# High and low parts of a weight unit side by side: a weight read at a stride of 8 bytes

## The chip, the cores and the metric

The kernel runs on one NeuronCore of a Trainium2 chip. The metric is the device time of one execution in microseconds. TensorE does the matmuls, VectorE, ScalarE and GpSimd prepare their operands and take over their results, and SyncE starts the DMAs.

## The reference

A two-layer encoder trunk works on two sequences of 256 tokens with 1024 features, 512 tokens in all, which share the weights. In fp32, each layer computes

```
h = x + 1/2 * SwiGLU(RMSNorm(x))            # feed-forward, 1024 -> 2816 -> 1024
u = RMSNorm(h); p = u @ w_in                # 28 tiles of 128 columns
A = retention(4 heads), B = differential attention(4 heads)
h = h + concat(A, B) @ w_out
h = h + 1/2 * SwiGLU(RMSNorm(h))            # second feed-forward
x = RMSNorm(h)
```

with `SwiGLU(x) = (silu(x @ wg) * (x @ wu)) @ wd`. Everything is fp32, and the result is compared as such. Nearly all the work is the products with weights.

## The kernel before

Activations lie transposed in SBUF: 128 features on the partitions, tokens along the row. A weight *unit* is 128 output columns times up to 8 tiles of 128 input rows, that is 128 partitions x 1024 words, 512 KB. Units stream in by DMA from SyncE's queue, in a written order, into four raw buffers (`raw`, and `raw_x` in the feed-forwards).

TensorE multiplies in the fast form fp32r, which rounds its operands. So each operand is split into a high part (the rounded value) and a low part (the rest), and each weight tile takes three matmuls, in `three` (L785 to L790): high weight times high moving tile (L788), high weight times low moving tile (L789), low weight times high moving tile (L790). Each of them loads its 128 x 128 weight tile anew, during the matmul before it. ScalarE writes the high part with a Copy from fp32 to fp32r; GpSimd or VectorE subtracts it from the raw value and writes the low part.

There are two kinds of units. *Plain* units are used in the first four products of each feed-forward, in its last down projection, in the 28 projections and in `w_out`. ScalarE splits one in L1276 and GpSimd in L679, in two halves. Most of their matmuls have 512 moving columns; the last products of the kernel are done for 256 tokens at a time, with 256 columns. *Fast blocks* make up the rest of the feed-forwards: 28 in each of four. A block takes two units (two gate/up units or two down units) as a 2 x 2 block matrix and computes it with seven half-size products instead of eight, p1 to p7, each of 4 tiles x 3 matmuls of 256 columns: 84 matmuls. For this the engines form sums and differences of weight quarters: per block, GpSimd runs L688 (low part of the first unit), L698 and L700 (differences of quarters, in place), L713 (low part of one quarter) and L706 (low part of two differences). ScalarE writes high parts in L1293, L1301, L1307, L1323 and L1330; VectorE writes two low parts in L1881. In some blocks GpSimd also runs L720, which concerns no weight.

Each engine's order is written out by hand, with semaphores between them. In GpSimd's order for block b come L713 and L706 of block b + 1 and then L688, L698 and L700 of block b + 2. L706 waits for L1301, which waits for L700 of its block. ScalarE's copies wait until TensorE has finished with the slot that they overwrite.

Split weights lie in slots. Slots 0 to 3 are in `w`, slots 4 and 5 in `w_x`; a fast block uses slots 0, 1, 2 or 3, 4, 5, alternately. `w_tiles` gives the high and low part of a slot: today two dense areas, the low part `W_PART` or `X_PART` words behind the high one, with the fourth slot 64 words further on (`SPACER`). Plain units begin 8 words (`PLAIN_AT`) later than the units of fast blocks (`block_tiles`). Moving operands are dense, with 256 or 512 words read in a row.

Of the kernel before, what the change touches and what calls it, by code (L numbers as in the profile page):

```python
# [30 lines left out]
F32R = mybir.dt.float32r  # L31
# [4 lines left out]
P = 128  # L36
# [18 lines left out]
UT = 8  # L55
SLOTS = 4
# [5 lines left out]
KH = KD // 2  # L62
PLAIN_AT = 8
SPACER = 64
W_AT = (0, UT * P, 2 * UT * P, 3 * UT * P + SPACER)
W_PART = SLOTS * UT * P + SPACER
X_PART = 2 * UT * P
GAP = 56


# [135 lines left out]
def build(nc, x, w_gu, w_dn, w_p, w_o, par, lam_vec, table, one_hot, cossin, rel, ident_in, centre_in, y):  # L206
    with ExitStack() as ctx:
        def sb(name, shape, dt=F32):
            return ctx.enter_context(nc.sbuf_tensor(name, shape, dt))
# [12 lines left out]
        a_lo = sb("a_lo", [P, UT, T], F32R)  # L222
        raw = sb("raw", [P, RAW * UT * P])
        pr = sb("pr", [P, N_PAR])
        w = sb("w", [P, 2 * W_PART + PLAIN_AT], F32R)
        acc = sb("acc", [P, T])
        rms = sb("rms", [P, T])
        cs = sb("cs", [P, 2, T])
# [21 lines left out]
        with ExitStack() as ffn_only:  # L250
            def sb_ffn(name, shape, dt=F32):
                return ffn_only.enter_context(nc.sbuf_tensor(name, shape, dt))

            raw_x = sb_ffn("raw_x", [P, RAW * UT * P])
            w_x = sb_ffn("w_x", [P, 2 * X_PART + PLAIN_AT], F32R)
            mix_hi = sb_ffn("mix_hi", [P, 3, KH, SEQ], F32R)
            mix_lo = sb_ffn("mix_lo", [P, 3, KH, SEQ], F32R)
            up = sb_ffn("up", [P, T])
            p1_copy = sb_ffn("p1_copy", [P, SEQ])
            u2 = sb_ffn("u2", [P, SEQ])  # L260
            u43 = sb_ffn("u43", [P, 2, SEQ])
            s14_h = sb_ffn("s14_h", [P, JS, T], F32R)
            s14_l = sb_ffn("s14_l", [P, JS, T], F32R)
            s2_h = sb_ffn("s2_h", [P, JS, SEQ], F32R)
            s2_l = sb_ffn("s2_l", [P, JS, SEQ], F32R)
# [225 lines left out]

        def w_tiles(s, n=UT, at_=0, shift=PLAIN_AT):

            buffer, part, first = (w, W_PART, W_AT[s]) if s < SLOTS else (w_x, X_PART, (s - SLOTS) * UT * P)
            first += shift + at_ * P
            hi, lo = buffer[:, first:first + n * P], buffer[:, part + first:part + first + n * P]
            return hi.rearrange("p (a b) -> p a b", b=P), lo.rearrange("p (a b) -> p a b", b=P)

        def block_tiles(s, n=UT, at_=0):

            return w_tiles(s, n, at_, 0)

        def w_tile(s, k):
            return w_tiles(s, 1, k)[0][:, 0, :]

        def w_low_tile(s, k):
            return w_tiles(s, 1, k)[1][:, 0, :]
# [1972 lines left out]
```

## Time and profile before

| | |
|---|---|
| median of 3 runs | 1840.61 us (1840.57 to 1845.08) |
| profiled execution | 1838.56 us, of which the span is 1836.8 us |
| TensorE busy | 99% of the span, 12744 matmuls |
| weight loads | 92% |
| VectorE, GpSimd, ScalarE busy | 75%, 73%, 55% |
| granted TensorE clock | 0.999 |
| DMA | 186.73 MB, 102 GB/s on average |

Busy times are unions of records. Records of matmuls overlap, since a matmul's record reaches to the end of its passage through the array; so the rate of TensorE is read from the distance between the starts of two matmuls, not from the mean duration of one.

### The profile page before, as it was taken

The numbers are of one execution on the slowest core, as the hardware profiler recorded it, in microseconds if no ns is written. First come the engines' busy times: TensorE is split into PE (matmuls) and PEld (weight loads), VectorE is DVE, ScalarE is ACT, GpSimd is POOL, SyncE is SP. The second block draws the span as 40 slices with busy tenths as digits, with TensorE's granted clock in tenths as the row PEclk, the third lists the DMA queues.
The fourth block names the chain that finished last, engine by engine and source line by source line (L and its number), as shares of the span: only waits on it lengthen the run. The fifth ranks groups of instructions, "written<-read, shape, count | busy, mean of one in ns | idle before, by whom it ended". The sixth has DMA issues, their size and how long they took to land. (4 is left out here: it accounts for less than half of the span.)

```text
span 1836.8 us, 33605 instructions
## 1 busy us (share of the span) xinstructions
PE 1822.8 (99%) x12744; PEld 1691.9 (92%) x12744; DVE 1375.7 (75%) x2409; ACT 1017.8 (55%) x1770; POOL 1348.4 (73%) x880
## 2 busy tenths in 40 slices
PE   9999999999999999999999999999999999999998
PEld 8999999887888999999889999998778889999997
DVE  7888886656755887887688888767477468888874
ACT  7656555456435665655575465555564266555553
POOL 6999897455445898988479998955544368999883
PEclk9999999999999999999999999999999999999999
DMA  4433333222223233323234233323222133333332
GB/s 153 151 110 122 115 118 107 85 99 69 69 69 114 72 114 115 108 101 110 80 110 139 96 112 116 100 86 115 80 69 70 58 115 98 110 116 106 102 113 72
DMA packets 56461, 186.73 MB, mean 102 GB/s; under 512 B 6600, under 2 KB 10440, under 8 KB 56300
## 3 DMA queue, kind: packets, MB, share of 16 engines
q1 hardware_dynamic: 54000, 181.09, 29.5%
q10 hardware_dynamic: 2300, 3.48, 0.5%
q8 instruction: 102, 1.67, 0.4%
q14 instruction: 59, 0.48, 0.1%
HBM read 182.44 MB, written 3.15 MB: 101 GB/s over the span
## 5 line engine op out<-in xcount | busy, mean ns | idle before, releaser
L788 PE MATMUL bank<-hg_hi,w 128*128 128x256 f32 (+1 forms) x1396 | 441.8, 317 | 0.1
L789 PE MATMUL bank<-hg_lo,w 128*128 128x256 f32 (+1 forms) x1396 | 438.3, 314 | 0.0
L790 PE MATMUL bank<-hg_hi,w 128*128 128x256 f32 (+1 forms) x1396 | 438.0, 314 | 0.0
L679 POOL TENSOR_TENSOR w<-raw,w 128x512 fp32r<-128x512 f32 (+1 forms) x194 | 259.1, 1358 | 217.7 <-ACT w L1276 217.6
L788 PEld LDWEIGHTS bank<-hg_hi,w 128*128 128x128 f32 x1396 | 262.2, 188 | 19.8 <-issue 2.7
L790 PEld LDWEIGHTS bank<-hg_hi,w 128*128 128x128 f32 x1396 | 262.3, 188 | 17.6
L789 PEld LDWEIGHTS bank<-hg_lo,w 128*128 128x128 f32 x1396 | 262.3, 188 | 16.9
L1356 ACT ACTIVATE bank<-bank 128x512 f32<-128x512 f32 x88 | 51.1, 581 | 237.5 <-DVE bank L1938 237.5
L1276 ACT ACTIVATE w<-raw 128x1024 fp32r<-128x1024 f32 (+1 forms) x97 | 98.8, 1023 | 120.6 <-PE bank L790 95.6
L706 POOL TENSOR_TENSOR w<-raw_x,w 128x1024 fp32r<-128x1024 f32 x56 | 135.0, 2411 | 26.2 <-ACT w L1301 26.2
L688 POOL TENSOR_TENSOR w<-raw_x,w 128x1024 fp32r<-128x1024 f32 x56 | 136.1, 2430 | 15.9 <-ACT w L1293 15.4
L706 POOL TENSOR_TENSOR w_x<-raw,w_x 128x1024 fp32r<-128x1024 f32 x56 | 135.2, 2414 | 14.0 <-ACT w_x L1301 14.0
L788 PE MATMUL bank<-a_hi,w 128*128 128x256 f32 (+1 forms) x472 | 139.7, 296 | 0.2 <-DVE a_lo L1865 0.2
L789 PE MATMUL bank<-a_lo,w 128*128 128x256 f32 (+1 forms) x472 | 139.0, 295 | 0.0
L790 PE MATMUL bank<-a_hi,w 128*128 128x256 f32 (+1 forms) x472 | 139.0, 294 | 0.0
L688 POOL TENSOR_TENSOR w<-raw,w 128x1024 fp32r<-128x1024 f32 x56 | 136.6, 2439 | 0.0
L788 PE MATMUL bank<-mix_hi,w_x 128*128 128x256 f32 x480 | 134.2, 280 | 2.1 <-DVE u L1907 2.1
L788 PE MATMUL bank<-mix_hi,w 128*128 128x256 f32 x480 | 134.1, 279 | 1.0 <-DVE w L1881 0.5
L789 PE MATMUL bank<-mix_lo,w 128*128 128x256 f32 x480 | 134.2, 279 | 0.0
L789 PE MATMUL bank<-mix_lo,w_x 128*128 128x256 f32 x480 | 134.2, 279 | 0.0
L790 PE MATMUL bank<-mix_hi,w 128*128 128x256 f32 x480 | 134.1, 279 | 0.0
L790 PE MATMUL bank<-mix_hi,w_x 128*128 128x256 f32 x480 | 134.0, 279 | 0.0
(345 smaller groups left out, 5824.2 us busy)
## 6 DMA issues: line engine op xcount, KB each, us to landing
raw<-in_w_gu SPq DMA_DIRECT2D x96, 512.0 KB, 4.0
raw_x<-in_w_gu SPq DMA_DIRECT2D x80, 512.0 KB, 4.3
raw<-in_w_p SPq DMA_DIRECT2D x56, 512.0 KB, 3.3
raw_x<-in_w_dn SPq DMA_DIRECT2D x32, 512.0 KB, 4.1
raw<-in_w_dn SPq DMA_DIRECT2D x32, 512.0 KB, 4.2
raw<-in_w_o SPq DMA_DIRECT2D x16, 512.0 KB, 3.3
raw_x<-in_w_dn SPq DMA_DIRECT2D x16, 384.0 KB, 3.9
raw<-in_w_dn SPq DMA_DIRECT2D x16, 384.0 KB, 3.5
```

What stands on the lines that cost most here:

```text
L679: ins = pool.tensor_tensor(columns(lo_[:, part, :]), source[:, part.start * P:part.stop * P], columns(hi[:, part, :]).bitcast(F32), ALU.su ...
L688: pool.tensor_tensor(columns(lo_), raw_tiles(RAW_AT["t", m, 0], UT), columns(hi).bitcast(F32), ALU.subtract).then_inc(g_lo, 1)
L706: pool.tensor_tensor(columns(lo_).rearrange("p (a b) -> p a b", a=2), both, columns(hi).rearrange("p (a b) -> p a b", a=2).bitcast(F32), A ...
L788: pe.matmul(out, hi[:, 0, :], m_hi, start=first, stop=False)
L789: pe.matmul(out, hi[:, 0, :], m_lo, start=False, stop=False)
L790: return pe.matmul(out, lo_[:, 0, :], m_hi, start=False, stop=last)
L1276: act.activation(columns(hi), raw_tiles(RAW_AT["e", e], TILES_OF[e]), ACT.Copy).then_inc(hi_done, 1)
L1356: act.activation(gated, gated, ACT.Silu).then_inc(silu_done, 1)
```

## The change

The two areas are replaced by one per slot, of 2048 words. Word 0 is the first high word, word 1 the first low word, word 2 the second high word, and so on. High and low parts become views with a step of two words. So a weight load of 128 columns reads 128 words spread over 1024 bytes, where it read 512 bytes in a row; and the Copies and subtractions that write or read these parts do it at a step of two words too. No instruction, wait or DMA is added or removed. `w` becomes 64 words shorter, so that the tensors allocated after it lie 256 bytes lower; `w_x` keeps its size, and the start of each kind of unit within 256 bytes is kept.

```diff
-W_AT = (0, UT * P, 2 * UT * P, 3 * UT * P + SPACER)
-W_PART = SLOTS * UT * P + SPACER
-X_PART = 2 * UT * P
+UNIT = 2 * UT * P
+W_AT = (0, UNIT, 2 * UNIT, 3 * UNIT + SPACER)
@@
-        w = sb("w", [P, 2 * W_PART + PLAIN_AT], F32R)
+        w = sb("w", [P, SLOTS * UNIT + SPACER + PLAIN_AT], F32R)
@@
-            w_x = sb_ffn("w_x", [P, 2 * X_PART + PLAIN_AT], F32R)
+            w_x = sb_ffn("w_x", [P, 2 * UNIT + PLAIN_AT], F32R)
@@
         def w_tiles(s, n=UT, at_=0, shift=PLAIN_AT):
-            buffer, part, first = (w, W_PART, W_AT[s]) if s < SLOTS else (w_x, X_PART, (s - SLOTS) * UT * P)
-            first += shift + at_ * P
-            hi, lo = buffer[:, first:first + n * P], buffer[:, part + first:part + first + n * P]
-            return hi.rearrange("p (a b) -> p a b", b=P), lo.rearrange("p (a b) -> p a b", b=P)
+            buffer, first = (w, W_AT[s]) if s < SLOTS else (w_x, (s - SLOTS) * UNIT)
+            first += shift + 2 * at_ * P
+            both = buffer[:, first:first + 2 * n * P].rearrange("p (a b two) -> p a b two", b=P, two=2)
+            return both[:, :, :, 0], both[:, :, :, 1]
```

## Rows read from the trace of the kernel before

**Rows 1.** The page, parts 1 and 4: engines, and the chain that ended last.
```profile
PE 1822.8 (99%) x12744; PEld 1691.9 (92%) x12744; DVE 1375.7 (75%) x2409; ACT 1017.8 (55%) x1770; POOL 1348.4 (73%) x880
...
PE 44%; DVE 0%; ACT 0%; POOL 0%; issue 0%; DVEq 0%; ACTq 0%
```

**Rows 2.** Groups by shape, TensorE: count, busy us and mean ns, idle before.
```profile
L788 PE MATMUL bank<-hg_hi,w 128*128 128x256 f32 x960 | 267.8, 279 | 0.1
L788 PE MATMUL bank<-hg_hi,w 128*128 128x512 f32 x436 | 174.0, 399 | 0.0
...
L1207 PE MATMUL bank<-s,v 128*128 128x256 f32 x64 | 15.1, 379 | 0.0
...
L788 PE MATMUL pair<-hg_hi,w_x 128*128 128x512 f32 x32 | 12.6, 393 | 0.0
...
L788 PE MATMUL pair<-hg_hi,w 128*128 128x512 f32 x32 | 12.5, 389 | 0.0
```

**Rows 3.** Windows: length; busy us (instructions) of PE, PEld, DVE, ACT, POOL; clock; DMA.
```profile
700.00:800.00 100.00, 99.98 (x857) 99.81 (x856) 81.85 (x156) 57.81 (x100) 89.91 (x55) 1.00 0.32 108
```

**Rows 4.** Timeline of TensorE in a fast block: start, duration; nine matmuls.
```profile
302.11 0.28 PE L788 MATMUL bank<-hg_hi,w 128*128 128x256 f32 x1
...
303.04 0.28 PE L790 MATMUL bank<-hg_hi,w 128*128 128x256 f32 x1
```

**Rows 5.** Timeline of TensorE in a projection; seven matmuls.
```profile
368.30 0.39 PE L788 MATMUL bank<-hg_hi,w 128*128 128x512 f32 x1
...
369.66 0.39 PE L788 MATMUL bank<-hg_hi,w 128*128 128x512 f32 x1
```

**Rows 6.** Timeline of TensorE in the last products; eleven matmuls.
```profile
1824.24 0.28 PE L788 MATMUL bank<-a_hi,w 128*128 128x256 f32 x1
...
1825.44 0.28 PE L789 MATMUL bank<-a_lo,w 128*128 128x256 f32 x1
```

**Rows 7.** Source view of L800, its load of 4 columns: min/median/max ns.
```profile
L800 PEld LDWEIGHTS bank<-a_t,o_r x2: 77/78/80, 26.7 to 26.7; 32*4 32x4 f32 x2
```

**Rows 8.** The page, part 5: weight loads of L788.
```profile
L788 PEld LDWEIGHTS bank<-hg_hi,w 128*128 128x128 f32 x1396 | 262.2, 188 | 19.8 <-issue 2.7
```

**Rows 9.** Timeline of TensorE, fp32 matmuls of the retention part, merged.
```profile
488.98 1.89 PE L1207 MATMUL bank<-s,v 128*128 128x256 f32 x8
```

**Rows 10.** The page, part 5: GpSimd's L688 and L706.
```profile
L706 POOL TENSOR_TENSOR w<-raw_x,w 128x1024 fp32r<-128x1024 f32 x56 | 135.0, 2411 | 26.2 <-ACT w L1301 26.2
L688 POOL TENSOR_TENSOR w<-raw_x,w 128x1024 fp32r<-128x1024 f32 x56 | 136.1, 2430 | 15.9 <-ACT w L1293 15.4
...
L688 POOL TENSOR_TENSOR w<-raw,w 128x1024 fp32r<-128x1024 f32 x56 | 136.6, 2439 | 0.0
```

**Rows 11.** Timeline of GpSimd over two rounds.
```profile
631.52 2.39 POOL L688 TENSOR_TENSOR w<-raw,w 128x1024 fp32r<-128x1024 f32 x1
...
636.93 0.74 POOL L720 TENSOR_TENSOR s_l<-a_t,s_h 128x256 fp32r<-128x256 f32 x1 [0.20 <-ACT s_h L1352]
...
641.26 2.41 POOL L688 TENSOR_TENSOR w<-raw_x,w 128x1024 fp32r<-128x1024 f32 x1
...
646.45 1.29 POOL L713 TENSOR_TENSOR w<-raw_x,w 128x512 fp32r<-128x512 f32 x1
648.19 2.41 POOL L706 TENSOR_TENSOR w<-raw_x,w 128x1024 fp32r<-128x1024 f32 x1 [0.44 <-ACT w L1301]
650.55 2.41 POOL L688 TENSOR_TENSOR w<-raw,w 128x1024 fp32r<-128x1024 f32 x1
```

**Rows 12.** Timeline of ScalarE in a fast block.
```profile
652.40 0.60 ACT L1330 ACTIVATE w<-bank 128x512 fp32r<-128x512 f32 x1
...
656.35 1.04 ACT L1301 ACTIVATE w_x<-raw 128x1024 fp32r<-128x1024 f32 x1
```

**Rows 13.** Groups of VectorE: L1881.
```profile
L1881 DVE TENSOR_TENSOR w_x<-bank,w_x 128x512 fp32r<-128x512 f32 x112 | 76.6, 684 | 11.9 <-ACT w_x L1323 6.1 <-ACT w_x L1330 4.4
```

## The prediction

> **What bounds the kernel now.** I read the page first: TensorE is busy for 99% of the span, and every entry of the chain that ended last is a TensorE line; no other engine has a per cent of it [rows 1]. So only two things can move the time: the distance between two matmuls, or a producer that stops keeping up. Next I read the groups by shape: almost all the work is three matmuls per weight tile at L788 to L790, in a 256-column and a 512-column form [rows 2]. Busy time says little here, since the records overlap; the distance between starts is what counts.
>
> In the timeline that distance is as regular as a clock. In the fast blocks (256 columns) eight steps take 0.93 us, and over 100 us 857 matmuls start: 116.7 ns each [rows 3, 4]. In a projection (512 columns) six steps take 1.36 us: 226.7 ns [rows 5]. In the closing products (256 columns) ten steps take 1.20 us: 120.0 ns [rows 6]. The last two use the same kind of weight unit ("plain", eight words further on), so they give the rate of the moving stream: 226.7 - 120.0 = 106.7 ns for 256 more columns, one column per cycle at the 2.4 GHz level, which is granted throughout [rows 3]. What is left is a fixed part of 13.3 ns per plain matmul, and 116.7 - 106.7 = 10.0 ns in the fast blocks. It is worth a lot: 112 fast blocks (56 + 56 calls of L688) [rows 10] x 84 matmuls = 9,408, times 10.0 ns = 94 us; about 2,700 matmuls of 512 columns (12,744 less 9,552 of 256 columns and nearly 500 others) times 13.3 ns = 36 us; and 144 at the end.
>
> **Where the fixed part comes from.** Three readings. First, fast and closing matmuls have the same number of columns and differ in where the weights start; the fixed part is 10.0 against 13.3 ns. It depends on addresses, so it is not plain issue cost. Second, a weight load of 4 columns takes 78 ns and one of 128 takes 188 [rows 7, 8]: 110 ns for 124 columns, 0.89 ns each, about two cycles. So dense weights are read at some 4.5 to 4.8 bytes per ns, while the moving operand of the fp32r form is read at 4 bytes per 0.417 ns, 9.6 bytes per ns. The moving read overtakes the weight read's address pattern again and again during each load. Third, in the fp32 matmuls of the retention part, eight records of 256 columns take 1.89 us, the last of them 0.38: 1.51 / 7 = 216 ns [rows 2, 9]. There each column takes two cycles (213.3 ns for 256), both reads advance at one speed, and the fixed part is only 2.6 ns. That the two reads of TensorE disturb each other when their addresses advance at different speeds is my reading of these three; the trace has no row for an fp32r matmul with a strided weight.
>
> **The change part by part.** *Weight reads.* Nothing is added to or removed from any queue: the same matmuls, loads, waits and DMAs in the same order. A weight read now steps 8 bytes per column, 9.0 to 9.6 bytes per ns: the speed of the moving read. If the reading above holds, a load that collides once is pushed out of step and stays clear. Best end: the fixed part falls to the 2.6 ns of the fp32 row, that is to 109.3 ns in the fast blocks and 215.9 at 512 columns: 9,408 x 7.4 ns = 70 us, 2,700 x 10.7 ns = 29 us, 144 x 10.7 ns = 1.5 us; together 100 us on TensorE alone. Worst end: a load touches twice as many bytes' worth of memory, and the fixed part doubles: 9,408 x 10.0 + 2,844 x 13.3 ns = 94 + 38 = +132 us (+163 us if the fast blocks pay 13.3 ns too). No row decides between them; the fp32 row is the nearest in kind, so I take the gain, with doubt, as the chances show.
>
> *What then comes late.* GpSimd. Where it waits only for its hand-over from ScalarE, its round of five subtractions takes 9.29 us (from the L688 at 641.26 to the next at 650.55) [rows 11], against 84 x 116.7 ns = 9.80 us of TensorE. With TensorE at 84 x 109.3 ns = 9.18 us, GpSimd's round is the longer one. Rounds that also hold the low part of a sum (8 of 28 in each feed-forward) cost about 0.5 us more: 9.74 us, from 631.52 to 641.26, with L720 inside [rows 11]. So the fast blocks of one feed-forward can't go below 28 x 9.29 + 8 x 0.45 = 263.7 us, from 28 x 9.80 = 274.4: 10.7 us, four times 43 us, instead of 70. I take 40 for these, and of the 29 us at 512 columns two thirds, 19, since the attention stages also hold waits on VectorE and ScalarE that don't shrink. With 1 us at the end: 60 us.
>
> *GpSimd's own work.* L688, L706 and L713 now read the high part and write the low part at a stride of 8 bytes; 2.43 + 2.41 + 1.29 = 6.13 us of each block [rows 10, 11]. No row here has a strided GpSimd operand. Lower end 0 (nothing that would make it cheaper: the elements are the same, about 2.35 ns each). Upper end: two of the three streams cost double, 5/3 of 6.13, +4.1 us per block; less the cover of 9.80 - 9.29 = 0.51 us, 112 x 3.6 = +400 us. I take 0, as the cost per element of these lines is already several times that of one step of ScalarE, which moves 1,024 elements in 1.04 us [rows 12], so that the address step is not what limits it. The point from which it decides: 0.51 us is 8% of 6.13; beyond that each further per cent is 0.061 x 112 = 7 us.
> The Trainium skill has a rule on this ("GPSIMD Engine Reference", section 7, Performance pitfalls for Q7 kernels): reads get half as dear again once the step exceeds 8 bytes. A step of 8 is just inside, so by that rule the cost is 0; it says nothing of writes, and no row here shows either.
>
> *ScalarE and VectorE.* L1293 and L1301 (1,024 elements, 1.04 us) and L1307, L1323 and L1330 (512, 0.60 us) write strided: 3.9 us of a block in which ScalarE is busy 58% [rows 3, 12]. L1881 reads and writes strided, 2 x 0.68 us, VectorE busy 82% [rows 3, 13]. On ScalarE 512 more elements cost 0.44 us, 0.86 ns each. I take 0; the upper end, twice the time, would put 1.04 us more of L1301 straight before L706, whose wait of 0.44 us for it is already there [rows 11]: GpSimd's round 10.33 us, less the 9.80 of TensorE, 0.53 x 112 = +59 us. The DMAs are unchanged, at a share of 0.32 [rows 3]. The weight tensor shrinks by 64 words, so all buffers behind it move by 256 bytes; units at both parities of 256 bytes exist today (w_x against w), with means of 393 and 389 ns [rows 2]; the 4 ns are the wait of a first tile, so I take 0, and as the upper end those 4 ns on all 512-column matmuls, 11 us.
>
> **Sum.** 1838.6 us (the profiled execution, 1836.8 of span) - 60 = 1778.6; the median of the runs shown is 2.0 us above the profiled one. I say 1779.
>
> **The rivals.** *A, the weight reads get dearer (slower).* The disturbance goes by the memory a load touches, not by relative speed. For it: the fixed part of plain units is 13.3 ns, 32 cycles, at 256 and at 512 columns alike, as a toll per load would be; the fp32 row can be explained by slack in its slower moving stream instead. Against it: the 10.0 ns for units only 32 bytes away. Price, as above: 1839 + 132 = 1971, up to 2002. It decides as soon as the mean distance in the fast blocks passes 116.7 ns, because TensorE has no idle time there; each further ns is 9.4 us.
> *B, nothing happens on TensorE.* The fixed part has to do with the load's start address and the switch of weights, and a step of 8 bytes is no burden. For it: the starts stay where they were, modulo 256 bytes. Against it: 116.7 and 120.0 ns for equal columns, and the 2.6 ns of fp32 [rows 4, 6, 9]. 1836 to 1841.
> The Trainium skill ("TensorE: Matmul & The Clock Gate", section Step-by-step: what each phase is for) speaks for B: TensorE has two independent read ports, one for each operand. By that there would be nothing to win or lose, 1839; the 116.7 against 120.0 ns for equal columns already speaks against full independence. "SBUF — State Buffer", section Specifications (TRN2), gives lines of 16 bytes and full rate from two hits per line; a step of 8 bytes has just two, so that rule sees no loss either, and A would contradict it.
> *C, strided producers (slower).* As bounded above; with GpSimd 20% dearer, (0.20 x 6.13 - 0.51) x 112 = +80, 1919; if TensorE wins at the same time, the same round still decides.
>
> **How the numbers follow.** Forecast 0.43, A 0.29, B 0.14, C 0.14. The forecast's own range is 1745 (GpSimd's round shortens a little as well, all of the 29 us come) to 1815 (half of the gain). Measurements of this kernel tell 0.3%, 5.5 us, from no change. Faster is the forecast, 0.43; same is B, 0.14; slower is A and C, 0.43. The range must reach into A and C: 1748 to 1975 leaves out the dearer half of A, some dear cases of C and a little below, not quite 2 in 10.
>
> **What would show it.** Distances in the fast blocks: 109 to 112 ns where GpSimd doesn't hold them up (A: 127 or more; B: 116.7). In a projection: 216 to 220 ns (A: 240; B: 226.7). Weight loads of 188 ns staying within 5. GpSimd's L706 at 2.41, L688 at 2.40 us (C: from 2.6 up), and new idle time of TensorE ended by POOL L706 or L713, with GpSimd above 95% in the fast blocks. I am wrong if TensorE's distances don't fall, or if a producer's mean rises by over 8%.

## The result, and the profile after

The changed kernel takes 1884.46 us (median of 3 runs, 1883.66 to 1884.89) against 1840.61 before: ratio 1.0239 [1.0224, 1.0253], 44 us slower. The forecast was 1779 us. The sign was wrong. The time lies inside the range of 1748 to 1975 only because that range was drawn to reach into the rivals; it is on the side of rival A, but far below A's 1971. Ratios, here and below, leave out executions that took over 1.5% more than the fastest of their kernel, which matters in E7 alone.

First the page of the changed kernel, its parts 1 and 4; the lines of the three matmuls are one earlier than before (L787 to L789).

```profile
PE 1867.8 (99%) x12744; PEld 1739.3 (92%) x12744; DVE 1380.6 (73%) x2409; ACT 1059.2 (56%) x1770; POOL 1370.6 (73%) x880
...
PE 43%; DVE 0%; ACT 0%; POOL 0%; issue 0%; DVEq 0%; ACTq 0%
```

TensorE still fills the span, so nothing has turned into a wait: the waits of TensorE that the changed kernel's trace lists are as small as before, and the two longest are these (line waited for: us in total, times, longest).

```profile
PE bank L787 <- DVE u L1906: 2.6, 3, 1.2
PE bank L851 <- ACT hg_hi L1738: 1.6, 1, 1.6
```

What grew is the distance between matmuls, from the start of one to the start of the next. The same 100 us as in [rows 3] (length; busy us and instructions of PE, PEld, DVE, ACT, POOL; clock; DMA), and the timeline of TensorE in a fast block (nine matmuls from the first row to the second), in a projection (seven) and in the last products (eleven):

```profile
700.00:800.00 100.00, 100.00 (x836) 100.00 (x835) 80.96 (x155) 57.74 (x93) 90.34 (x55) 1.00 0.32 107
```
```profile
311.33 0.28 PE L787 MATMUL bank<-mix_hi,w_x 128*128 128x256 f32 x1
...
312.29 0.29 PE L789 MATMUL bank<-mix_hi,w_x 128*128 128x256 f32 x1
...
376.17 0.40 PE L787 MATMUL bank<-hg_hi,w 128*128 128x512 f32 x1
...
377.57 0.39 PE L787 MATMUL bank<-hg_hi,w 128*128 128x512 f32 x1
...
1859.85 0.28 PE L787 MATMUL bank<-a_hi,w 128*128 128x256 f32 x1
...
1861.05 0.28 PE L788 MATMUL bank<-a_lo,w 128*128 128x256 f32 x1
```

In the fast block eight steps take 0.96 us, 120.0 ns each (before 116.7, [rows 4]); in 100 us 836 matmuls start where 857 did. In the projection six steps take 1.40 us, 233.3 ns (before 226.7, [rows 5]). In the last products ten steps take 1.20 us, 120.0 ns, just as before [rows 6]: a first hint that a stride alone is no toll on every load. Averaged over all neighbouring starts of the two traces, the distances (those under 160 and 300 ns) go from 116.9 to 120.4 ns at 256 columns and from 227.4 to 233.1 at 512: 9,408 x 3.5 + 2,700 x 5.7 ns = 33 + 15 = 48 us, against the 45 us by which the span grew (1836.8 to 1881.9). The other 3 us are the breaks in the 256-column stream: what its distances above 160 ns hold beyond the regular pace falls from 10.0 to 6.7 us, since a slower TensorE waits less. The granted clock is 0.999 before and after, so cycles and not the clock explain it.

The other rows that answer to those of before: the weight load, GpSimd's two large subtractions, ScalarE's L1301 (now L1300) and VectorE's L1881 (now L1880).

```profile
L787 PEld LDWEIGHTS bank<-hg_hi,w 128*128 128x128 f32 x1396 | 273.4, 196 | 19.5 <-issue 2.6
L705 POOL TENSOR_TENSOR w<-raw_x,w 128x1024 fp32r<-128x1024 f32 x56 | 138.2, 2467 | 30.6 <-ACT w L1300 30.6
L687 POOL TENSOR_TENSOR w<-raw_x,w 128x1024 fp32r<-128x1024 f32 x56 | 138.8, 2479 | 17.9 <-ACT w L1292 17.9
...
L1300 ACT ACTIVATE w_x<-raw 128x1024 fp32r<-128x1024 f32 x56 | 64.6, 1153 | 0.0
...
L1880 DVE TENSOR_TENSOR w_x<-bank,w_x 128x512 fp32r<-128x512 f32 x112 | 76.7, 685 | 18.6 <-ACT w_x L1329 11.5 <-ACT w_x L1322 7.2
```

A weight load takes 196 ns instead of 188 [rows 8]. GpSimd's rows grow by 2%, from 2430 and 2411 [rows 10] to 2479 and 2467; ScalarE's by 10%, from 1050 ns on average (L1301 into `w_x`) to 1153; VectorE's not at all (684 to 685, [rows 13]).

### The profile page after: what moved, and what is told of

Same layout as the page of the kernel before. It is cut to its first block and busy times, and to the rows that moved or that the text cites. A ratio compares the mean times of both kernels' runs of the same rounds, so it can differ in the third digit from the quotient of the medians.

```text
span 1881.9 us, 33605 instructions
## 1 busy us (share of the span) xinstructions
PE 1867.8 (99%) x12744; PEld 1739.3 (92%) x12744; DVE 1380.6 (73%) x2409; ACT 1059.2 (56%) x1770; POOL 1370.6 (73%) x880
## 5 line engine op out<-in xcount | busy, mean ns | idle before, releaser
L787 PE MATMUL bank<-hg_hi,w 128*128 128x256 f32 (+1 forms) x1396 | 449.1, 322 | 0.0
L788 PE MATMUL bank<-hg_lo,w 128*128 128x256 f32 (+1 forms) x1396 | 445.2, 319 | 0.0
L789 PE MATMUL bank<-hg_hi,w 128*128 128x256 f32 (+1 forms) x1396 | 445.0, 319 | 0.0
L678 POOL TENSOR_TENSOR w<-raw,w 128x512 fp32r<-128x512 f32 (+1 forms) x194 | 266.4, 1398 | 223.4 <-ACT w L1275 223.2
L787 PEld LDWEIGHTS bank<-hg_hi,w 128*128 128x128 f32 x1396 | 273.4, 196 | 19.5 <-issue 2.6
L789 PEld LDWEIGHTS bank<-hg_hi,w 128*128 128x128 f32 x1396 | 273.2, 196 | 17.2
L788 PEld LDWEIGHTS bank<-hg_lo,w 128*128 128x128 f32 x1396 | 273.4, 196 | 16.6
L1275 ACT ACTIVATE w<-raw 128x1024 fp32r<-128x1024 f32 (+1 forms) x97 | 107.1, 1109 | 125.8 <-PE bank L789 98.6
L705 POOL TENSOR_TENSOR w<-raw_x,w 128x1024 fp32r<-128x1024 f32 x56 | 138.2, 2467 | 30.6 <-ACT w L1300 30.6
L687 POOL TENSOR_TENSOR w<-raw_x,w 128x1024 fp32r<-128x1024 f32 x56 | 138.8, 2479 | 17.9 <-ACT w L1292 17.9
L705 POOL TENSOR_TENSOR w_x<-raw,w_x 128x1024 fp32r<-128x1024 f32 x56 | 138.0, 2465 | 18.0 <-ACT w_x L1300 16.4
L787 PE MATMUL bank<-a_hi,w 128*128 128x256 f32 (+1 forms) x472 | 142.2, 301 | 0.0
L788 PE MATMUL bank<-a_lo,w 128*128 128x256 f32 (+1 forms) x472 | 141.4, 299 | 0.0
L789 PE MATMUL bank<-a_hi,w 128*128 128x256 f32 (+1 forms) x472 | 141.3, 299 | 0.0
L787 PE MATMUL bank<-mix_hi,w_x 128*128 128x256 f32 x480 | 136.8, 285 | 1.7 <-DVE u L1906 1.7
L787 PE MATMUL bank<-mix_hi,w 128*128 128x256 f32 x480 | 136.9, 285 | 0.9 <-POOL w L705 0.6
L789 PE MATMUL bank<-mix_hi,w 128*128 128x256 f32 x480 | 136.7, 285 | 0.0
L788 PE MATMUL bank<-mix_lo,w 128*128 128x256 f32 x480 | 136.6, 285 | 0.0
L789 PE MATMUL bank<-mix_hi,w_x 128*128 128x256 f32 x480 | 136.6, 285 | 0.0
L788 PE MATMUL bank<-mix_lo,w_x 128*128 128x256 f32 x480 | 136.6, 285 | 0.0
```

What stands on the lines that cost most here:

```text
L678: ins = pool.tensor_tensor(columns(lo_[:, part, :]), source[:, part.start * P:part.stop * P], columns(hi[:, part, :]).bitcast(F32), ALU.su ...
L687: pool.tensor_tensor(columns(lo_), raw_tiles(RAW_AT["t", m, 0], UT), columns(hi).bitcast(F32), ALU.subtract).then_inc(g_lo, 1)
L705: pool.tensor_tensor(columns(lo_).rearrange("p (a b) -> p a b", a=2), both, columns(hi).rearrange("p (a b) -> p a b", a=2).bitcast(F32), A ...
L787: pe.matmul(out, hi[:, 0, :], m_hi, start=first, stop=False)
L788: pe.matmul(out, hi[:, 0, :], m_lo, start=False, stop=False)
L789: return pe.matmul(out, lo_[:, 0, :], m_hi, start=False, stop=last)
```

## The experiments

All starts are those of the weights, in words modulo 64 (256 bytes), counted from where the moving operands start. Before the change the plain units start at 0 and the fast blocks' at 56; the change keeps both. Except in the two kernels of measurements, an edit is shown against the kernel before (E4 to E8) or against the changed one (E1 to E3, E9); times are medians, beside 1839.6 to 1841.5 us for the kernel before on the same chips.

### The reads measured by themselves (M1)

One line per case, 32 matmuls each, with the number of columns, the weights' start and step and the moving operand's step as its only variables; then Copies and subtractions alone. It ran once, with a granted clock of 1.00 over the first 440 us of its span, where all cases of TensorE used here lie.

```diff
+for i in range(REP): pe.matmul(acc[:, 0:256], wts(64, 1, 1), mv[:, 0:256], start=True, stop=True)
+for i in range(REP): pe.matmul(acc[:, 0:256], wts(120, 1, 1), mv[:, 0:256], start=True, stop=True)
+for i in range(REP): pe.matmul(acc[:, 0:256], wts(64, 2, 1), mv[:, 0:256], start=True, stop=True)
+for i in range(REP): pe.matmul(acc[:, 0:256], wts(64, 1, 1), mvs(256, 2), start=True, stop=True)
```

> This kernel computes nothing of the reference; it measures the disputed cost by itself. TensorE runs 70 settings of 32 equal fp32r matmuls each, 256 or 512 moving columns, with the weight read at a step of 1, 2, 3, 4 or 8 words and its start moved by 0 to 56 words against the moving operand, in some settings the moving operand at a step of 2 words; nothing else runs. Then ScalarE, GpSimd and VectorE copy or subtract 1024 elements at steps of 1 and 2 words, alone, and ScalarE once more beside TensorE. Theory 'toll' (a load that walks over more memory holds the moving read up longer, wherever it starts): at step 2 all eight starts give about 233 ns at 512 columns and 120 ns at 256, at step 4 and 8 clearly more (over 245 and 130), dense 226.7 and 116 to 120. Rival 'phase' (the fixed part goes by the distance of the two addresses): at step 2 the starts differ among themselves by more than 5 ns and at least one is at or below the best dense one (226.7 and 116.7). Rival 'relative speed', the one of the prediction: the smallest distance at every moving step comes where the weight step is twice the moving one's speed in words, so moving step 2 with weight step 4 is faster than with 1 or 2. ScalarE at a write step of 2: 1.15 us against 1.04 alone as well, if the stride costs; 1.04 if it was only the company of the other engines. GpSimd 2.47 against 2.41 with either the read or the write strided.

Its timeline of TensorE gives one row per case (start, time of all 32, line). 256 columns with dense weights at start 0 and 56; weights at step 2, start 0 and 56; step 3; step 4; then the moving operand at step 2 with weights at step 1, 2 and 4:

```profile
28.46 4.07 PE L74 MATMUL acc<-mv,wt 128*128 128x256 f32 x32
...
58.14 3.98 PE L88 MATMUL acc<-mv,wt 128*128 128x256 f32 x32
...
62.31 4.09 PE L90 MATMUL acc<-mv,wt 128*128 128x256 f32 x32
...
92.41 4.09 PE L104 MATMUL acc<-mv,wt 128*128 128x256 f32 x32
...
126.72 5.80 PE L120 MATMUL acc<-mv,wt 128*128 128x256 f32 x32
...
138.72 7.72 PE L124 MATMUL acc<-mv,wt 128*128 128x256 f32 x32
...
170.92 7.50 PE L132 MATMUL acc<-mv,wt 128*128 128x256 f32 x32
...
178.62 7.60 PE L134 MATMUL acc<-mv,wt 128*128 128x256 f32 x32
...
186.43 7.89 PE L136 MATMUL acc<-mv,wt 128*128 128x256 f32 x32
```

A row holds 31 distances and the last matmul's own passage, so 0.10 us between two rows is 3.2 ns per matmul; the distances below are those of the last 16 matmuls of a row. Dense, 256 columns: 120.0 at start 0, 116.7 at 56. Step 2: 120.0 at both. So the isolated read shows what the kernel showed, without any producer. The low parts of the changed kernel start one word after the high ones; M1 has that start as well (65), and it takes 120.0 ns too. The forecast's theory falls on the last three rows: with the moving operand at step 2, weights at step 4 are the slowest (236.5 ns), and weights at the same step 2 (230.0) are slower than dense ones (226.7). The expectation had put the match at step 4, for a moving read of one column per cycle. It takes two (226.7 ns for 256 columns), so the equal speed is at step 2; neither helps. Rival A's doubled toll falls too: at 256 columns step 2 adds 0 to 3.3 ns and not 10. At 512 columns it adds 6.6 ns at start 0 (226.7 to 233.3), nothing at 56 (233.4 both) and takes 3.3 off at 16 (233.3 to 230.0). The cost does come, but only past step 2: 173.4 ns at step 3, 233.4 at step 4.

The groups of weight loads in the same run, for step 1 (L88), 2 (L90), 3 (L120) and 4 (L124), and the subtractions of GpSimd: dense, one operand read at step 2, result written at step 2, both, read at step 3; last the Copies of ScalarE: 1,024 elements dense, written at step 2, and 512 elements dense, written at step 3 and 4.

```profile
L88 PEld LDWEIGHTS acc<-mv,wt 128*128 128x128 f32 x32 | 3.8, 188 | 0.0
...
L90 PEld LDWEIGHTS acc<-mv,wt 128*128 128x128 f32 x32 | 3.9, 196 | 0.0
...
L120 PEld LDWEIGHTS acc<-mv,wt 128*128 128x128 f32 x32 | 5.6, 261 | 0.0
...
L124 PEld LDWEIGHTS acc<-mv,wt 128*128 128x128 f32 x32 | 7.6, 330 | 0.0
```
```profile
L61 POOL TENSOR_TENSOR sc<-src,sc 128x1024 fp32r<-128x1024 f32 x4 | 9.3, 2337 | 564.2 <-ACT sc L234 564.0
L62 POOL TENSOR_TENSOR sc<-src,sc 128x1024 fp32r<-128x1024 f32 x4 | 9.5, 2369 | 0.3
L63 POOL TENSOR_TENSOR sc<-src,sc 128x1024 fp32r<-128x1024 f32 x4 | 9.4, 2342 | 0.3
L64 POOL TENSOR_TENSOR sc<-src,sc 128x1024 fp32r<-128x1024 f32 x4 | 9.6, 2388 | 0.3
L65 POOL TENSOR_TENSOR sc<-src,sc 128x1024 fp32r<-128x1024 f32 x4 | 10.3, 2573 | 0.3
```
```profile
L224 ACT ACTIVATE sc<-src 128x1024 fp32r<-128x1024 f32 x4 | 4.2, 1056 | 526.6 <-PE acc L214 526.5
L225 ACT ACTIVATE sc<-src 128x1024 fp32r<-128x1024 f32 x4 | 4.5, 1116 | 0.1
L231 ACT ACTIVATE sc<-src 128x512 fp32r<-128x512 f32 x4 | 2.5, 629 | 0.1
L226 ACT ACTIVATE sc<-src 128x512 fp32r<-128x512 f32 x4 | 3.5, 877 | 0.1
L227 ACT ACTIVATE sc<-src 128x512 fp32r<-128x512 f32 x4 | 4.4, 1100 | 0.1
```

The producers' stride costs GpSimd 2% (2337 to 2388) and ScalarE 6% (1056 to 1116); VectorE's four cases take 1225 to 1226 ns all. Beside a busy TensorE the Copy pays the same 6% (1059 to 1126 ns). A cost of 2% on GpSimd is below the 8% from which rival C decides.

### The layout without the stride (E1), and the stride in one kind of unit (E2, E3)

E1 keeps the change's one area per slot but puts high and low part densely behind each other in it. E2 does so where `shift == 0`, the fast blocks, so that only plain units are interleaved; E3 does it where `shift != 0`.

```diff
 buffer, first = (w, W_AT[s]) if s < SLOTS else (w_x, (s - SLOTS) * UNIT)
+if True:                      # E2: shift == 0, E3: shift != 0
+    first += shift + at_ * P
+    hi, lo = buffer[:, first:first + n * P], buffer[:, UT * P + first:UT * P + first + n * P]
+    return hi.rearrange("p (a b) -> p a b", b=P), lo.rearrange("p (a b) -> p a b", b=P)
```

> The changed layout with one thing undone: each slot still has one area of 2048 words and every buffer lies where the change put it, but within the slot the high part is 1024 dense words and the low part the 1024 behind them. If the stride costs (toll, phase): back to the kernel before, 1841 us within 5, distances 116.7, 226.7 and 120.0 ns, ScalarE's L1301 at 1.05 us. If the move of the later buffers by 256 bytes costs: it stays near 1884 us.

> Only the plain units are interleaved, fast blocks are dense within their slots. Toll: 512-column matmuls at 233.3 ns, +5.8 ns on 2,700, +16 us and some more at their breaks: 1857 us. If the sum of this and the next run falls short of the change's 44 us, the layouts of the two kinds interact. Phase says the same here.

> Only the units of the fast blocks are interleaved. 9,408 matmuls at about 120 to 121 ns instead of 116.9, +28 to +34 us: 1870 us. If ScalarE's or GpSimd's dearer strided work were the cause and not TensorE's reads, TensorE would show idle time ended by L1301's or L706's line, and the 512-column stages of the run before would be free.

| | time, us | ratio | distance at 512, 256 columns, ns |
|---|---|---|---|
| E1 | 1839.82 | 1.0005 [0.9996, 1.0015] | 227.4, 117.1 |
| E2 | 1856.00 | 1.0088 [1.0073, 1.0103] | 233.1, 117.1 |
| E3 | 1869.68 | 1.0163 [1.0148, 1.0178] | 227.4, 120.5 |

(Distances are means over neighbouring starts of each trace.) Moving the buffers costs nothing. At the starts that the kernel uses, the stride costs 16 us in the plain units and 30 us in the fast blocks, together 46 against the 44 of both at once, and each kind of unit changes its own distance only. E3's row for the window of [rows 3]:

```profile
700.00:800.00 100.00, 100.00 (x829) 100.00 (x828) 79.76 (x152) 58.78 (x94) 89.70 (x54) 1.00 0.31 106
```

### Every start (M2)

M1 left a doubt: the dense distances themselves moved with the start, from 116.7 to 120.0 and from 226.7 to 234.3 ns. So a second kernel, which like M1 computes nothing of the reference, goes through all 64 dense starts and the even starts at step 2, 30 matmuls each, in the kernel's order of three.

```diff
+for i in range(10): [pe.matmul(acc[:, 0:256], a, m, start=True, stop=True)
+    for a, m in ((wts(80, 1), mv[:, 0:256]), (wts(80, 1), mv[:, 512:768]), (wts(1104, 1), mv[:, 0:256]))]
```

> Computes nothing of the reference. TensorE runs 192 settings of 30 fp32r matmuls in the kernel's own order (high weight x high, high weight x low, low weight x high), dense weights at each start from 0 to 63 words modulo 64 and step-2 weights (high and low interleaved) at each even start, for 256 and 512 moving columns. If the distance goes by the start (phase): dense at 512 columns has its minimum of 226.7 ns near start 0 and lies at 231 to 234 elsewhere, dense at 256 its minimum near 56; step 2 lies between 230 and 234, and between 118 and 122, with no start as good as the best dense one. If instead every setting of one step is alike within 1 ns, the start doesn't matter and the toll is the stride's own.

It ran once too, with a granted clock of 1.00. Timeline of TensorE, 30 matmuls a row: 256 columns dense at start 0, 16 and 56; step 2 at start 20. Then 512 columns: dense at 0, 39 and 56; step 2 at 0 and 26.

```profile
27.64 3.84 PE L66 MATMUL acc<-mv,wt 128*128 128x256 f32 x30
...
91.50 3.67 PE L98 MATMUL acc<-mv,wt 128*128 128x256 f32 x30
...
251.13 3.74 PE L178 MATMUL acc<-mv,wt 128*128 128x256 f32 x30
...
323.85 3.81 PE L214 MATMUL acc<-mv,wt 128*128 128x256 f32 x30
```
```profile
413.06 7.08 PE L258 MATMUL acc<-mv,wt 128*128 128x512 f32 x30
...
702.17 7.55 PE L336 MATMUL acc<-mv,wt 128*128 128x512 f32 x30
...
828.95 7.24 PE L370 MATMUL acc<-mv,wt 128*128 128x512 f32 x30
888.25 7.24 PE L386 MATMUL acc<-mv,wt 128*128 128x512 f32 x30
...
984.68 7.15 PE L412 MATMUL acc<-mv,wt 128*128 128x512 f32 x30
```

| distance, ns | best | mean of the starts | worst | at the start that the kernel uses |
|---|---|---|---|---|
| 256, dense | 113.3 (13, 16, 19, 22, 42) | 118.3 | 121.1 (6) | 116.9 (56) |
| 256, step 2 | 118.3 (60) | 120.1 | 123.3 | 120 (56) |
| 512, dense | 226.7 (0, 30, 33) | 232.6 | 243.3 (39) | 226.7 (0) |
| 512, step 2 | 229.9 (26, 28) | 232.2 | 233.5 | 233.3 (0) |

(Distances over the last 18 matmuls of a row.) The kernel before sits on a good start in both forms, in the 512-column form on the best one. At step 2 the starts differ less, and none of them is as good as the dense 226.7 and 116.7 of the kernel before. At 512 columns the two means are alike, 232.6 and 232.2. At start 0 the 256-column form takes 120 ns dense or not, which is why the last products did not move.

### Dense units at other starts (E4, E5)

If the good starts are what was lost, the kernel before must lose most of the same time with no stride at all. E4 moves the plain units from 0 to 56, E5 the fast blocks from 56 to 0.

```diff
-PLAIN_AT = 8
+PLAIN_AT = 0                                  # E4, buffers as large as before
@@
-            return w_tiles(s, n, at_, 0)
+            return w_tiles(s, n, at_, PLAIN_AT)   # E5, in block_tiles
```

> The kernel before, dense, with plain units starting 8 words earlier, at 56 words modulo 64 against the moving operand instead of 0. Phase: 512-column matmuls go from 226.7 to 233.4 ns as in the first reads table, 2,700 x 6 ns = +16 us, 1856 us, the same as with strided plain units (1856.0); the closing 256-column ones go from 120.0 to 116.7. Toll (the stride itself costs): unchanged, 1840 us.

> The kernel before, dense, with the units of fast blocks starting 8 words later, at 0 modulo 64. Phase: 256-column matmuls at 120.0 ns instead of 116.9, 9,408 x 3.1 ns = +29 us, 1869 us, the same as with strided blocks (1869.7). Toll: unchanged, 1840 us.

E4: 1853.68 us, ratio 1.0072 [1.0057, 1.0087], +13.6 where the stride cost 16.4; its 512-column distance is 233.2 ns. Its last products, plain units of 256 columns, go from 119.9 to 116.7 ns, as expected. E5: 1863.16 us, 1.0124 [1.0107, 1.0140], +23 where the stride cost 30; its distance in the fast blocks is 120.0 ns. That is the expected distance, +29 us for 9,408 matmuls; E5 stays 6 us below its expected 1869 mostly because the breaks of the stream shrank from 10.0 to 5.5 us. First a projection of E4 on the timeline (six steps, 1.40 us), then E5 in the window of [rows 3] and its weight load:

```profile
376.45 0.39 PE L788 MATMUL bank<-hg_hi,w 128*128 128x512 f32 x1
...
377.85 0.39 PE L788 MATMUL bank<-hg_hi,w 128*128 128x512 f32 x1
```
```profile
700.00:800.00 100.00, 100.00 (x835) 100.00 (x834) 79.76 (x152) 55.92 (x94) 89.32 (x55) 1.00 0.33 106
```
```profile
L788 PEld LDWEIGHTS bank<-hg_hi,w 128*128 128x128 f32 x1396 | 265.4, 190 | 19.7 <-issue 2.7 <-DVE w L1881 0.2
```

Dense reads at a poorer start look almost like strided ones: 835 matmuls in 100 us against 836 in the changed kernel.

### Better starts (E6 to E9)

The table promises 113.3 ns for some dense starts. E6, E7 and E8 put the fast blocks at 16, 13 and 42 and keep the plain units at 0; E9 puts the interleaved units at starts that are among the best of step 2, 20 in the fast blocks and 26 in the plain units. A head in front of `w` and `w_x`, another `PLAIN_AT` and a smaller gap do it, with the buffers longer by as much, so that the moving operands keep their places; E6's edit, without the buffers' sizes:

```diff
-PLAIN_AT = 8
+PLAIN_AT = 48
+W_HEAD, X_HEAD = 24, 0
@@
-GAP = 56
+GAP = 16
@@
-            first += shift + at_ * P
+            first += shift + at_ * P + (W_HEAD if s < SLOTS else X_HEAD)
```

> The kernel before, dense, with only starts moved: units of fast blocks start at 16 words modulo 64 against the moving operands instead of 56, plain units stay at 0, and the moving operands keep their places. The table of starts has 113.3 ns there (in the kernel's order of three). Phase: 9,408 x (116.9 - 113.3) = -34 us; GpSimd's round of 9.29 us (9.74 with L720) against 84 x 113.3 = 9.52 us takes back a few: 1810 us. If the table's 113.3 was a settling that depends on how a stretch begins (the first table, with one operand pair alone, had 117.8 at 16): 1840 to 1850 us. Toll (no influence of the start): 1840.

> As the run before, with fast blocks at 13 words modulo 64, where the table has 113.3 ns as well: 1810 us by the phase theory, 1840 and more if the table's value doesn't last in the kernel. An odd word start costs ScalarE and GpSimd nothing as far as the tables show.

> Fast blocks at 42 words modulo 64, a third start with 113.3 ns in the table, between neighbours of 118 to 120: 1810 us by the phase theory, 1855 to 1870 if only the neighbourhood counts.

> The changed kernel, interleaved, with the best starts that the table has for a step of 2: fast blocks at 20 (118.5 ns) and plain units at 26 (229.9 ns). Phase: against 1884, 9,408 x 1.9 ns = -18 and 2,700 x 3.2 ns = -9 us: 1857 us; what stays above 1840 is the stride's own toll, 9,408 x 1.6 + 2,700 x 2.5 = 22 us. Toll alone: 1884, wherever the units start.

| | time, us | ratio | distances in the fast blocks, ns |
|---|---|---|---|
| E6, dense, 16 | 1826.33 | 0.9909 [0.9885, 0.9932] | 113.3 in 461 stretches, 117.8 in 269 |
| E7, dense, 13 | 1820 to 1855; one 2240 at clock 0.752 | 0.9957 [0.9905, 1.0010] | 120.0 in 484, 113.3 in 213, 117.8 in 41 |
| E8, dense, 42 | 1869.42 | 1.0154 [1.0139, 1.0169] | 120.0 in 743, 113.3 in 7 |
| E9, step 2, 20 and 26 | 1863.99 | 1.0123 [1.0108, 1.0138] | 120.0 in 225, 117.8 in 318 |

(A stretch is twelve matmuls, and its distance the mean of the twelve steps to the next stretch; there are 784, and only the commonest values are listed. The kernel before has 116.7 in 586 and 117.8 in 147.) E6 is the fastest of all kernels here. Its timeline shows both patterns, on either side of a wait: twelve steps between the first two rows, 1.36 us, and between the last two, 1.41 us.

```profile
790.64 0.28 PE L789 MATMUL bank<-a_hi,w 128*128 128x256 f32 x1
...
792.00 0.28 PE L789 MATMUL bank<-a_hi,w 128*128 128x256 f32 x1
...
792.86 0.36 PE L789 MATMUL bank<-s_h,w_x 128*128 128x256 f32 x1 [0.35 <-DVE u L1908]
...
793.29 0.28 PE L789 MATMUL bank<-s_h,w_x 128*128 128x256 f32 x1
...
794.70 0.28 PE L789 MATMUL bank<-a_hi,w 128*128 128x256 f32 x1
```

So the same weights at the same start can run in one of several settled rhythms. Laid out in order of time, the stretches also show when a rhythm changes. In the traces of the kernel before, E6, E7 and E8 it never changes from one stretch directly to the next. Between two rhythms there always lies a stretch in which the even sequence is broken by a long distance, often a wait of TensorE; in E6 it is 188 ns to 1.6 us long. The rhythm of E6 differs across 15 of 27 such breaks, and between them it holds for up to 82 stretches, 984 matmuls. Each row of M2 starts anew after other matmuls, so it may be one draw of several.

E6 keeps the best rhythm about 60% of the time, E7 under 30% in the execution that was profiled (1854.82 us), E8 hardly ever; E7 can't be told from no change. Two things keep E6 from its expected 1810 us: its mean distance is 115.1 ns and not 113.3, which gives 17 us of the 34 expected, and the breaks of its stream grow from 10 to 15 us. E8 misses its sign because its start hardly ever holds the rhythm that its row of M2 showed. E9 was expected at 1857 and wins back 20 of the 44 us: its distances are as expected (118.7 and 230.1 ns on average), and its breaks grow by 4 us against the changed kernel. The best that I found for interleaved units is still 38 us above the best for dense ones.

## Why the prediction was wrong

**The step that failed** is the first of its sum: "If the reading above holds, a load that collides once is pushed out of step and stays clear. Best end: the fixed part falls to the 2.6 ns of the fp32 row." It rose instead, from 10.0 to 13.3 ns in the fast blocks and from 13.3 to 20 ns at 512 columns. The reading behind it, that the operands disturb each other when their addresses advance at different speeds, is refuted by M1: equal speeds (both at step 2) gave 230.0 ns, unequal ones (dense weights) 226.7. The changed kernel refutes it too, since its two reads advance at equal speed as the prediction reckoned it. The three observations were sound, and the first, that the fixed part depends on the start, was the one to follow; I put it down to speed because of the fp32 row. What makes the 2.6 ns of that row stays open. Rival A put it down to slack, since a column there takes two cycles. M1 speaks against slack alone: with the moving operand at step 2 a column takes about two cycles as well, the weights are dense, and the fixed part is still 226.7 - 213.3 = 13.4 ns.

**What took its place.** The fixed part depends on where the weights start, dense or strided, and on the rhythm. That the start counts without any stride is shown in the kernel: E4 and E5 lose 37 of the 46 us that the stride cost, with dense weights. How much is left for the stride itself is an estimate, and depends on which dense start one compares with. From M2's averages, with 9,408 and 2,700 matmuls: at 512 columns going from the tuned start to an average dense one costs 232.6 - 227.4 = 5.2 ns, 14 us, and the stride on top nothing (232.2). At 256 columns the start accounts for 118.3 - 117.1 = 1.2 ns, 11 us, and the stride for 120.1 - 118.3 = 1.8 ns, 17 us. That makes some 25 us for the lost start and 17 for the stride, of 44. The kernels point the same way at 256 columns: the mean distances at the five dense starts timed (56, 0, 16, 13, 42) are 117.0, 120.0, 115.1, 117.8 and 119.9 ns, 118.0 on average, and at the two strided ones (56, 20) 120.4 and 118.7. In M2 no interleaved start reaches the dense 116.7 and 226.7 ns, so the change had nothing to win at any start tried, as far as one row per start can tell.

**Rival A** had the right sign, and the load did get longer (188 to 196 ns), but it was mis-sized and only in part the cause: I doubled the fixed part, +10.0 and +13.3 ns; measured were +3.5 and +5.7. Doubling was the end of a range with no row behind it. The last products, 120.0 before and after, show that a load 8 ns longer need not cost anything. In M1 a load of 330 ns (step 4) leaves 235.0 ns per matmul at 512 columns, but 233.4 at 256, where dense weights take 120.0: there the load sets the pace.

**Rival B** was wrong on TensorE, though its sentence, that the fixed part has to do with the load's start, was the true one. I concluded from "the starts stay where they were" that the distance stays, but a start's value is not the same for a strided read: start 0 is the best of the 512-column dense starts and among the poorer ones at step 2 (233.3 ns, of 229.9 to 233.5). The rule cited for B, two independent read ports ("TensorE: Matmul & The Clock Gate", section Step-by-step: what each phase is for, of the Trainium skill), gives no reason for 226.7 to 243.3 ns by the weights' start alone; that the two reads get in each other's way is not shown by that either. The rule of two hits per 16-byte line ("SBUF — State Buffer", section Specifications (TRN2), of the Trainium skill) fits the loads better: 196 ns at step 2, then 261 and 330 at step 3 and 4, and the same knee in ScalarE's writes, 877 and 1100 ns for the 629 of 512 dense elements. It does not fit the moving operand: at step 2, with two hits per line, 256 columns take 226.7 ns for 120.0.

**Rival C** did not happen: GpSimd +2%, below the 8% from which it decides, and no new wait of TensorE for L705 or L712. My 0 for the producers was right where it mattered and wrong for ScalarE, which pays 0.10 us per Copy of 1,024 elements, 10% and so past the 8% that the prediction named as a sign; at 56% busy that stays hidden while TensorE needs 120 ns per matmul. In M1 the Copy pays 0.06 us alone and 0.07 beside TensorE, so TensorE's company is not what makes it 0.10 in the kernel; what does stays open. The rule on steps above 8 bytes ("GPSIMD Engine Reference", section 7, Performance pitfalls for Q7 kernels, of the Trainium skill) was right that a step of 8 bytes is harmless; past it, with one of two operands read at 12 bytes, I measured +10% (2573 against 2337 ns) and not half as much again.

**The other terms.** The shift of all buffers by 256 bytes, taken at 0, is 0 (E1, within 0.15%). TensorE as the only bound was right: the matmul counts times the distances give 48 us, less 3 us of shorter breaks. The limit by GpSimd's round never came into play.

**Still open** is why a start is good and which rhythm a break leaves behind. The numbers show that the weights' start matters and that several rhythms are stable at one start; they name no bank or port. Only weights were moved, so it is not shown whether their own address counts or its distance from the moving operand's. Nor is it shown what share the load's own pace has at 256 columns: by [rows 7, 8] a column of weights takes 0.89 ns, some 114 ns for 128 columns as an estimate, close to the best distance of 113.3. A load of fewer columns was not tried.

## What to carry to other kernels

When TensorE is the bound, measure the distance from one matmul to the next for every start address of the weights before you change their layout, and afterwards again: a layout has its own best start, and a new one tried at the old start is judged unfairly. A toll per matmul of 3 ns that no record shows is 2% of such a kernel. Take a distance from a microbenchmark as a candidate only; which rhythm a long stretch settles into has to be timed in the kernel, as E6 and E8 show, and it can be another one after each break of the stream.

## What the runs showed of the hardware

- The distance of fp32r matmuls with a new load each depends on the weights' start in SBUF: dense, 113.3 to 121 ns at 256 columns, 226.7 to 243.3 at 512 in M2, and 117.0 against 120.0 ns (the kernel before and E5) over thousands of matmuls.
- Weights at step 1, 2, 3, 4 (of 4 bytes) load in 188, 196, 261, 330 ns; at 256 columns the last two are no longer hidden (173.4, 233.4 ns per matmul).
- An fp32r moving operand read at step 2 takes about two cycles per column: 226.7 ns for 256 columns with dense weights, where a dense moving operand takes 120.0.
- The same sequence of matmuls at the same start runs in different settled rhythms (E6: 113.3 and 117.8 ns), which changed only across a break of the stream (at 15 of 27 breaks). Another dense start of the fast blocks alone is worth from -15 us (E6) to +28 us (E8) in this kernel.
